# Row norms tile by tile: half-row squares, a shorter root, rows scaled and then turned

## What is computed

```python
def rms_norm(x, g):
    y = xf * lax.rsqrt(jnp.mean(xf * xf, axis=-1, keepdims=True) + NORM_EPS)
    return (y * g).astype(x.dtype)

for i in range(DEPTH):                         # first block
    h = rms_norm(x, ln_attn_g[i])              # a0, a1
    ...
    x = x + jnp.concatenate([y_diff, y_moba], axis=-1) @ w_out[i]
    x = x + conv_ffn(rms_norm(x, ln_ffn_g[i]), ...)      # f0, f1
for l in range(DEPTH):                         # second block
    h_l = _rmsnorm(x, g_pre[l]) * (1.0 + sc_l) + sh_l    # x0, x1
    h_c = _rmsnorm(xc, g_pre[l]) * (1.0 + sc_c) + sh_c   # c0, c1
    ...
    xc = xc + gt_c * _rmsnorm(out_c, g_post[l])          # layer 0 only
    x = x + gt_l * _rmsnorm(out_l, g_post[l])
```

## Time and profile before

| | us |
|---|---|
| median of 3 runs | 2309.98 |
| lowest, highest | 2309.71, 2314.76 |
| the profiled execution's own time | 2309.95 |
| its span in the trace | 2307.9 |
| PE busy | 2138.2 (93%) |
| DVE, ACT, POOL busy | 1321.8, 963.7, 555.7 |

### The profile page before, as it was taken

How to read it: one execution, slowest core, us unless ns; L and a number is a source line. 1 busy time by engine, 2 the same in 40 slices (tenths; PEclk the granted TensorE clock), 3 DMA queues, 4 the chain that set the end, 5 groups by cost and what they waited for, 6 DMA issues and landing times.

```text
span 2307.9 us, 31382 instructions
## 1 busy us (share of the span) xinstructions
PE 2138.2 (93%) x12074; PEld 1829.8 (79%) x12074; DVE 1321.8 (57%) x2200; ACT 963.7 (42%) x1602; POOL 555.7 (24%) x323
## 2 busy tenths in 40 slices
PE   7888998988999899999999999999989788989998
PEld 6668897766999688877887788888768688878997
DVE  5735666674777415638434456867361667565464
ACT  4434554443555424353323453232342553435443
POOL 1413333242333311011211002322231111320432
PEclk9979999988999999999999999999989899999999
DMA  9334665321455422212122115534323323341543
GB/s 250 126 136 167 232 217 201 128 91 65 160 180 190 133 92 73 82 46 73 65 95 87 47 37 175 182 102 138 120 78 126 101 83 110 110 147 46 174 146 129
DMA packets 79066, 285.00 MB, mean 123 GB/s; under 512 B 8822, under 2 KB 9730, under 8 KB 78920
## 3 DMA queue, kind: packets, MB, share of 16 engines
q1 hardware_dynamic: 70560, 256.15, 32.8%
q10 hardware_dynamic: 6072, 18.73, 2.3%
q0 software_dynamic: 2288, 8.13, 1.3%
HBM read 277.14 MB, written 5.83 MB: 123 GB/s over the span
## 4 chain that ended last, share of the span: by engine, by line
PE 40%; DVE 9%; ACT 4%; issue 2%; POOL 0%; POOLq 0%; DVEq 0%; ACTq 0%
PE pb L830 8%; PE pb L832 8%; PE pb L831 8%; PE pb L842 3%; PE pb L844 3%; PE pb L843 3%; PE pb L848 2%; PE pb L1156 2%; PE pb L1137 1%; ACT SPH L1277 1%; DVE GW L2105 1%; DVE SPL L1815 1%; PE pb L1053 1%; PE pb L1097 1%; DVE ATT L2133 1%
## 5 line engine op out<-in xcount | busy, mean ns | idle before, releaser
L1815 DVE TENSOR_TENSOR SPL<-RAW,SPH 128x1024 fp32r<-128x1024 f32 (+1 forms) x291 | 416.2, 1437 | 479.5 <-ACT SPH L1277 443.2
L2392 POOL TENSOR_TENSOR SPL<-RAW,SPH 128x1024 fp32r<-128x1024 f32 x171 | 418.6, 2450 | 1112.4 <-ACT SPH L1277 998.8
L830 PE MATMUL pb<-HTH,SPH 128*128 128x256 f32 (+1 forms) x1984 | 647.0, 326 | 8.1 <-DVE SPL L1815 3.9
L831 PE MATMUL pb<-HTL,SPH 128*128 128x256 f32 (+1 forms) x1984 | 636.9, 321 | 0.0
L832 PE MATMUL pb<-HTH,SPL 128*128 128x256 f32 (+1 forms) x1984 | 636.7, 321 | 0.0
L1277 ACT ACTIVATE SPH<-RAW 128x1024 fp32r<-128x1024 f32 x462 | 476.6, 1048 | 287.7 <-PE pb L844 130.2
L830 PEld LDWEIGHTS pb<-HTH,SPH 128*128 128x128 f32 x1984 | 381.7, 192 | 42.5 <-issue 14.1
L831 PEld LDWEIGHTS pb<-HTL,SPH 128*128 128x128 f32 x1984 | 382.1, 193 | 26.9
L832 PEld LDWEIGHTS pb<-HTH,SPL 128*128 128x128 f32 x1984 | 381.5, 192 | 27.1
L842 PE MATMUL pb<-SPH,HTH 128*128 128x512 f32 x544 | 222.0, 408 | 18.5 <-DVE SPL L1815 8.8
L844 PE MATMUL pb<-SPL,HTH 128*128 128x512 f32 x544 | 217.0, 399 | 0.0
(11 more groups left out here) (271 smaller groups left out, 2957.9 us busy)
## 6 DMA issues: line engine op xcount, KB each, us to landing
RAW<-in_w_up SPq DMA_DIRECT2D x88, 512.0 KB, 4.3
RAW<-in_wa SPq DMA_DIRECT2D x64, 512.0 KB, 3.2
RAW<-in_w_in SPq DMA_DIRECT2D x48, 512.0 KB, 5.3
RAW<-in_wmg SPq DMA_DIRECT2D x48, 512.0 KB, 3.2
RAW<-in_wbr SPq DMA_DIRECT2D x48, 512.0 KB, 3.2
RAW<-in_w_down SPq DMA_DIRECT2D x44, 512.0 KB, 3.5
RAW<-in_w_ada SPq DMA_DIRECT2D x24, 512.0 KB, 4.8
ARAW<-in_w_ada ACTq DMA_DIRECT2D x24, 512.0 KB, 4.0
```

Of the source, the lines that this page charges most:

```text
L830: T.matmul(o, wh[:, kt, :], xh[:, kt, n0:n1], start=kt == 0, stop=False)
L831: T.matmul(o, wh[:, kt, :], xl[:, kt, n0:n1], start=False, stop=False)
L1815: W.tensor_tensor(lo, raw, hi.bitcast(F32), SUB).then_inc(*dve.tick(s["lo_dve"], ("u", u)))
L2392: G.tensor_tensor(lo, raw, hi.bitcast(F32), SUB).then_inc(*pool.tick(s["lo_pool"], ("u", u)))
```

## The change

- **Squares.** Steps `sq`: a tile's sum of squares is taken in two halves of 512 columns, on ACT, as soon as each half is ready (for a0 and c0 the second half on DVE).
- **Root.** One root per tile on 128x1: an operation on the first half's sum, then eight in a chain once the second half's sum is there (before: eleven for two tiles). The same for `x_out`.
- **Scaling, then turning.** DVE scales columns 0 to 511 of a tile by its root, ACT the rest (for tile 0 of f0 and f1 ACT scales all), into XN. Steps `nt`: PE turns the 16 blocks of 128x128 by a transpose against the identity. Steps `nh`: HTH and HTL are written from PSUM. For x0, c0 and c1 ACT now writes HTH straight from PSUM, with DVE doing the scale and shift once more for the low part, and the low parts shared by DVE and POOL; x1 keeps its division of labour.
- **Last products tile by tile** (`group_by_tile`): the second output group of the attention, the last LAG = 3 down products, the first projection group of layer 1 (its tile 0 ahead of the turns of a1's tile 1) and the second w2 group, so that squares, roots and turns of one tile stand beside the products of another.
- **Second block, layer 0**: the group of context values gv comes first, context tiles ahead of x's tiles, with x0's turns between; the decay rank, gk and gq follow.
- Down products follow the up products by 3 tiles instead of 2, AH and AL have 4 buffers instead of 3. `ahead` puts splits on POOL. Loading TRI, the mask and the context moves from the start into the feed-forward network of layer 0. `x_half` multiplies by GB, `x_out` adds AFX to the first half in one operation with the scaling; XS goes out in four DMAs instead of two.

In all, PE has as many instructions as before, DVE 51 more, ACT 8 more; 9 weight splits go from DVE to POOL.

The core of the diff:

```diff
-PF = 2
+PF, LAG = 2, 3
...
+    def group_by_tile(self, key, name, g, tiles, src, both=0):
+        for i in range(both):
+            u = self.get_w(name, g * 4 + i)
+            self.add("gn", key, i, u, tiles, src, True)
+            self.put_w(u)
+            yield
+        us = [self.get_w(name, g * 4 + i) for i in range(both, 4)]
+        for t in tiles:
+            for i, u in enumerate(us):
+                self.add("gn", key, both + i, u, (t,), src, t == tiles[-1])
+                if t == tiles[-1]:
+                    self.put_w(u)
+                    self.ahead()
+                yield
+    def ahead(self):
+        was = list(self.split_on)
+        self.split_on[:] = (1,)
+        self.split_upto(self.gets - 1 + PF)
+        self.split_on[:] = was
+    def squares(self, tag, i):
+        for half in range(2):
+            self.add("sq", tag, i, half)
+    def root(self, tag, i):
+        self.add("root", tag, i, 0)
+        self.add("root", tag, i, 1)
+        self.add("xn", tag, i)
...
+    def qkv_first(self, ring):
+        for t in range(2):
+            self.take(ring, ("qkv", 1, 0, t))
+        for n, _ in enumerate(self.group_by_tile(("qkv", 1, 0), "w_in1", 0, (0, 1), ("a1",))):
+            if n == 3:
+                self.turns("a1", 1)
+                self.evict("a1", range(8), 1)
+            yield
...
+        tag = f"f{l}"
+        for t in range(2):
+            self.add("res1", l, 0, t)
+            self.give(("wo", l, 0, t))
+            self.add("sq", tag, t, 0)
+        for t in range(2):
+            self.take((2, 3), ("wo", l, 1, t))
+        for n, _ in enumerate(self.group_by_tile(("wo", l, 1), f"w_out{l}", 1, (0, 1), ("Y", l), 1)):
+            if n == 3:
+                self.add("res1", l, 1, 0)
+                self.give(("wo", l, 1, 0))
+                self.add("sq", tag, 0, 1)
+                self.add("root", tag, 0, 0)
+        self.add("res1", l, 1, 1)
+        self.give(("wo", l, 1, 1))
+        self.add("root", tag, 0, 1)
+        self.add("sq", tag, 1, 1)
+        self.add("xn", tag, 0)
+        self.root(tag, 1)
+        self.nt_take(tag, HI4)
+        for i in range(2):
+            self.turns(tag, i)
...
+    def down_end(self, l):
+        tag, first = "x0" if l else "a1", FF_TILES - LAG
+        us = [self.get_w(f"w_down{l}", first + i) for i in range(LAG)]
+        for i, t in ((0, 0), (1, 0), (0, 1), (2, 0), (1, 1), (2, 1)):
+            self.add("down", l, first + i, us[i], (t,))
+            if t:
+                self.put_w(us[i])
+                self.ahead()
+            if (i, t) == (2, 0):
+                for half in range(2):
+                    self.add("res2", l, 0, half)
+                    self.give(("dn", l, 0, half))
+                    self.add("sq", tag, 0, half)
+        self.root(tag, 0)
+        for half in range(2):
+            self.add("res2", l, 1, half)
+            self.give(("dn", l, 1, half))
+        if l:
+            self.squares(tag, 1)
+            self.root(tag, 1)
+            return
+        self.nt_take(tag, LO4, 0)
+        self.turns(tag, 0)
+        self.evict(tag, range(4), 0)
...
+            for t in (2, 3):
+                self.take(ALL8, ("gv", l, 0, t))
+            self.nt_take("x0", ALL8)
+            for t in (0, 1):
+                self.take(ALL8, ("gv", l, 0, t))
+            for n, _ in enumerate(self.group_by_tile(("gv", l, 0), f"wgv{l}", 0, (2, 3, 0, 1), H)):
+                if n == 3:
+                    for i in range(2):
+                        self.turns("x0", i)
+                    self.evict("x0", range(8))
+                    self.add("spill_x")
+                    self.add("wdec", l)
+            values(0)
...
+                t = tlist[n // 4]
+                self.add("x_out", l, t)
+                self.give(("w2", l, 1, t))
+                if not last and t < 2:
+                    self.squares("x1", t)
+                    self.root("x1", t)
+            elif not last and n == 13:
+                self.nt_take("x1", LO4)
+                for i in range(2):
+                    self.turns("x1", i)
+                self.evict("x1", range(4))
+                self.squares("c1", 0)
+                self.evict("x1", range(4, 6))
+        if last:
+            return
+        self.evict("x1", range(6, 8))
+        for n, _ in enumerate(self.gla_queries(1, ("x1",))):
+            if n == 0:
+                self.root("c1", 0)
+            elif n == 1:
+                self.squares("c1", 1)
+                self.root("c1", 1)
+        self.nt_take("c1", ALL8)
+        for i in range(2):
+            self.turns("c1", i)
+        self.evict("c1", range(8))
...
+    def sq(tag, i, half):
+        if half and tag in SQUARED_BY_DVE:
+            return
+        t, c = NORMS[tag][i], slice(half * 512, half * 512 + 512)
+        k.rows_ready(act, tag, t, half)
+        xn_free(act, k, tag, i)
+        A.activation(xn_tile(sb, tag, i)[:, c], sb["XS"][:, t, c], ACT.Square, scale=1.0,
+                     accum_out=sb["SS"][:, 2 * t + half:2 * t + half + 1]).then_inc(
+            *act.tick(s["norm_act"], ("sq", tag, i, half)))
+    def xn(tag, i):
+        t, c = NORMS[tag][i], slice(0 if (tag, i) in SCALED_BY_ACT else 512, 1024)
+        act.wait_ge(s["norm_dve"], ("rs", tag, i))
+        A.activation(xn_tile(sb, tag, i)[:, c], sb["XS"][:, t, c], ACT.Copy, scale=sb["NW"][:, i, 8:9]).then_inc(
+            *act.tick(s["norm_act"], ("xn", tag, i)))
...
+    def nt(tag, b, i):
+        P, x = bank(nt_bank(tag, b, i)), xn_tile(sb, tag, i)
+        for kt in (b, b + 4):
+            if kt < 4 and (tag, i) not in SCALED_BY_ACT:
+                pe.wait_ge(s["norm_dve"], ("xn", tag, i))
+            else:
+                pe.wait_ge(s["norm_act"], ("xn", tag, i))
+            at = nt_block(tag, kt, i)[0].start + (0 if tag in BY_TILE else i * 128)
+            m = turn(P[:, at:at + 128], x[:, kt * 128:(kt + 1) * 128])
+        m.then_inc(*pe.tick(mm, ("nt", tag, b, i)))
...
+    def root_step(signal, w, n, out, *names):
+        dve.wait_ge(*dve.last)
+        W.scalar_tensor_tensor(out=w[:, 7:8], in0=w[:, 6:7], scalar=w[:, n:n + 1], in1=w[:, 6:7], op0=MUL,
+                               op1=MUL).then_inc(*dve.tick(signal))
+        dve.wait_ge(*dve.last)
+        W.scalar_tensor_tensor(out=out, in0=w[:, 7:8], scalar=3.0 if n == 2 else -3.0, in1=w[:, 6:7], op0=ADD,
+                               op1=MUL).then_inc(*dve.tick(signal, *names))
...
+    def root(tag, i, part):
+        n, t, w = s["norm_dve"], NORMS[tag][i], sb["NW"][:, i, :]
+        if part == 0:
+            dve.wait_ge(s["norm_act"], ("sq", tag, i, 0))
+            root_open(n, w, sb["SS"][:, 2 * t:2 * t + 1])
+            dve.wait_ge(s["norm_dve" if tag in SQUARED_BY_DVE else "norm_act"], ("sq", tag, i, 1))
+            root_guess(n, w, sb["SS"][:, 2 * t + 1:2 * t + 2])
+            root_step(n, w, 0, w[:, 6:7], ("rp", tag, i))
+            return
+        dve.wait_ge(n, ("rp", tag, i))
+        root_step(n, w, 1, w[:, 6:7])
+        root_step(n, w, 2, w[:, 8:9], ("rs", tag, i))
...
         dve.wait_ge(*dve.last)
-        rsqrt(o, ("xr", l, t), SSO[:, 1, t:t + 1], SSO[:, 0, t:t + 1], 1.0 / 1024, 1)
-        dve.wait_ge(o, ("xr", l, t))
         dve.wait_ge(*k.read(("w2", l, 0, t)))
-        for hf in range(2):
-            dve.wait_ge(*k.read(("gr", l, t // 2, hf)))
-        W.scalar_tensor_tensor(out=x[:, 512:1024], in0=k.P(name)[:, :], scalar=SSO[:, 1, t:t + 1],
-                               in1=GB[:, t // 2, 512:1024], op0=MUL, op1=MUL).then_inc(*dve.free(*k.read(name)))
-        W.scalar_tensor_tensor(out=x[:, 0:512], in0=x[:, 0:512], scalar=SSO[:, 1, t:t + 1],
-                               in1=GB[:, t // 2, 0:512], op0=MUL, op1=MUL).then_inc(*dve.tick(o))
+        dve.wait_ge(s["x_back"], 16 * (l + 1))
+        W.scalar_tensor_tensor(out=x[:, 0:512], in0=x[:, 0:512], scalar=r, in1=sb["AFX"][:, t, 0:512], op0=MUL,
+                               op1=ADD).then_inc(*dve.tick(o, ("x", l, t, 0)))
+        dve.wait_ge(*k.read(("gr", l, t // 2, 1)))
+        W.scalar_tensor_tensor(out=x[:, 512:1024], in0=k.P(name)[:, :], scalar=r, in1=sb["GB"][:, t // 2, 512:1024],
+                               op0=MUL, op1=MUL).then_inc(*dve.free(*k.read(name)))
         dve.wait_ge(*dve.last)
-        dve.wait_ge(*k.read(name))
-        dve.wait_ge(s["x_back"], 16 * (l + 1))
-        W.tensor_tensor(x, x, sb["AFX"][:, t, :], ADD).then_inc(*dve.tick(o, ("x", l, t)))
+        W.tensor_tensor(x[:, 512:1024], x[:, 512:1024], sb["AFX"][:, t, 512:1024], ADD).then_inc(
+            *dve.tick(o, ("x", l, t, 1), ("x", l, t)))
```

563 lines of the change are left out of this document (285 added, 278 removed).

## The result

The changed kernel takes 2318.23 us (median of 10 runs, 2317.11 to 2320.08), the kernel before, run beside it, 2311.81 (10 runs, 2309.71 to 2314.76). The ratio is 1.0029, interval 1.0019 to 1.0039: slower by 0.29%. The forecast was 2287, its range 2274 to 2302. It was wrong in size and in direction.

The account below looks back on a forecast made before the run. PE's matmuls (busy 2138.2 of 2307.9 us) bound the kernel, so only idle and half clock could be won. 4.0 + 0.8 + 5.7 + 11.5 + 1.6 + 0.3 - 1.0 = 22.9; 2309.95 - 22.9 = 2287, range 2274 to 2302.

Parts of the forecast that it names:

- a1: Norm ahead of layer 1's projections: gain 0.8 us, bounds -2 and +8, with splits late behind the second tile's scaled rows.
- x0: Norm ahead of the second block: less PE idle and no wait for AL, gain 5.7 us, bounds 3 and 8.
- the end: After the last square: fewer root steps, a half-width addition and a smaller last DMA, gain 1.6 us.
- f0 and f1: Norms ahead of both layers' up products: shorter root path, 2.0 us each, 4.0 together, bounds 1 and 9.
- the start: Start with a0's norm: one transfer gone, POOL splits before building bias rows, gain 0.3 us, bounds -1 and +1.6.
- the network of layer 0: Feed-forward loops: LAG and the fourth AH/AL buffer change nothing, as long as PE stays at its 128x512 pitch.
- c0: Context norm, placed in layer 1's attention: extra DVE and ACT work, loss of 1.0 us, bounds -3 and +1.
- x1 with c1: Norms at the end of the first block 2 layer: query groups start earlier, gain 11.5 us, bounds 6 and 14.
- rival B: At a1, x0, f0, f1 and x1: splits come in time, clock holds, gains 36.9 us, 2273; chance 0.14.
- C: Rival: half clock behind the turns at f0, f1, a1, x0 and c1 loses 8 us, 2295; chance 0.18.
- E: Rival: slower, POOL's added splits hold DVE 21 us in dense stages, c0 adds 4.4, 2313; chance 0.05.
- same: Whole kernel: a time not distinguishable from no change, within about 0.3% (6.9 us); chance 0.07.

Follow-up runs that it names:

- e10: e5 with the TRI, mask and context loads back at the start and the mask's cast ahead of the attention: 2294.99 us.
- e1: Changed kernel with low parts after the first four weight splits on DVE until layer 0's attention, not every third on POOL: 2308.04 us.
- e2: Changed kernel with the doubled modulation steps of layer 0's feed-forward network at tiles 7 and 8 instead of 8 and 9: 2310.06 us.
- e3: Changed kernel with two more weight splits ahead of tile 1's squares and root at a1 and x0: 2305.98 us.
- e5: Changed kernel with the edits of e1, e2 and e3 together: 2286.56 us, ratio 0.9888 to the kernel before.
- e9: e5 with all of c0's norm moved from layer 1's projections and attention into its feed-forward network: 2276.74 us.
- e7: e5 with c0's column blocks written out one per step of the attention instead of two: 2286.12 us.
- e8: e5 with the two splits taken during the last w2 tile on DVE instead of POOL: 2284.74 us.
- e4: Changed kernel with plain products against the identity in place of the transposes: 2327.87 us.
- after: The changed kernel itself, without any follow-up edit: 2318.23 us, ratio 1.0029 to the kernel before.
- e6: e5 with one more split ahead of c0's squares and roots in layer 1's projections: 2287.10 us.

## Why the prediction was wrong, step by step

- **What bounds.** Held: with as many turns as products only idle and half clock could be won, and the DG waits went away in full. The prediction looked for gains in the holes that exist, and for losses mostly in the same places. It did not walk through the stages in which PE had no hole. Of the sum's terms a1, x0 and the end came out right, f0 and f1 under-sized; the start, the network of layer 0, c0, and x1 with c1 failed, and they are 7.4, 13.5, 6.9 and 7.1 us of error.
- **Start, 0.3, measured a loss of 7.1. The failed step** is "POOL splits before it builds the bias rows: 0.3". Two splits do stand ahead of the bias rows (10.51 and 22.79), but the costly two stand behind their round trip through DRAM (9.36 us). The trip was to be read in the trace of before (8.11 us of idle), and that splits now follow it from the new kernel's order. And the moved load, which the prediction took for one of several small things, is worth 9.6 (e10). Two terms of about ten, a cost (12.6, e1) and a gain, both put at next to nothing.
- **Feed-forward, "nothing, as long as PE stays at its 128x512 pitch", measured a loss of 13.5 in layer 0. The failed step, and the largest.** The condition was stated and not examined. The doubling at tiles 8 and 9 made PE wait 6.00 us for AROW; e2 took 8.2 us of it back by moving the doubling one tile. Another 4.2 are the loads and the mask's cast, moved here from the start (e10). Nothing in PE's pitch before could show it; the order of ACT and PE around tiles 8 and 9 would have.
- **f0 and f1, 4.0, measured 4.1 and 4.5, 8.6 together.** Mechanism right; under-sized by half. The first turn came at T + 3.2 and the first up product at T + 6.8 instead of 8.5 (T here the last output product). The mis-sized term is the evictions: the sum let them run to T + 8.5 ahead of the up products; they ran under them. And the transposes take 3.57 us, against 5.12 for the products, which the sum left out.
- **a1, 0.8, measured a loss of 0.2; x0, 5.7, measured 5.6.** Right place, right mechanism (splits behind the scaled rows on ACT), shown by e3: 5.7 and 4.9 us. For a1 the sum had T + 23.3 against 24.1; it came to 24.24 against 24.04. With the splits in time (e5) it is 5.5 and 12.0, rival B's direction.
- **c0, a loss of 1.0 with bounds -3 and +1, measured 7.9. Mis-sized term.** I added up c0's work (4.4 us on DVE and ACT), took a part of it, and placed it all in the attention, though its squares and roots stand in the projections (2.1 of the loss). There the chain of two roots and scalings occupies DVE from 445.37 to 451.66 and ACT waits with the next split; in the attention the turns wait another 6.24 for HVC. The work was not the price; the position in the order was. e9 gives back 9.8 by moving it. What inside the attention holds HVC stays open, since e7 did not settle it.
- **x1 and c1, 11.5, measured 4.4. Mis-sized term.** Tile 3 with the turns in it ended as forecast to 0.5 us (1689.4 against 1689.9). The last query copy is at 1730.41 - 14.6 = 1715.8, forecast 1707.5, a gain of 3.9 instead of 12.2; PE's own query products end 6.9 earlier, 5.3 less than forecast. Late low parts (POOL's splits are 2.5, e8), ACT's evictions and the clock at 0.50 until 1719.5 are what the traces show there; all were in the prediction's warnings, not in its sum. The step "c1's turns and evictions follow as before" failed too: the faster turns ran into a new wait of 4.02 us for c1's low parts, a net 2.7.
- **End, 1.6, measured 1.5.** Right.
- **The rivals.** C is refuted where it was looked at (e4, the windows of f0 and f1). E named a mechanism that exists (DVE held for 2.3 us beside a POOL split, and after's 1702.11) and an outcome on the right side; but e1 to e3 win back more than the whole loss elsewhere, without its 21 us of held DVE in the dense stages. e8 puts the one place where it was tried at 2.5 us. (By E's own figures eight held splits beside c0's 4.4 us are enough to reach no change, not ten, and the parts named for "same" add up to 0.085, not 0.07.) No rival held the two mechanisms that decided: a queue behind a round trip, and a producer and its consumer moved into one step.

Without the two faults of order (e1 and e2, 18.4 us measured singly) after would be at about 2300, inside the range; e5 has them out together with e3.

## What to carry to other kernels

- Of an engine that takes over work, read what stands ahead of the new work in its in-order list, waits included. A wait that cost nobody anything becomes everybody's when something needed is queued behind it.
- When a step is doubled or merged, look whether a producer on one engine and its consumer on another now fall into the same step; one step between them was worth 8 us here.
- A stage's price is not the added work but the delay of the next thing in the list that PE needs. Work that two other orders did not hide in a dense stage (e6, e7) could be put whole into a stage where PE is the bound (e9). Before stages of two kernels are compared between two products, the same work must lie ahead of both: here twelve products did not, which makes a1 look 2 us worse in the table and x0 1 us. A total that comes out right (e5, 2286.56 against 2287) proves no term of the sum.

## What the runs showed of the hardware

- A 128x128 float32 transpose is one record and a product of the same size two, at the same pitch: from the first of 16 to the next stage 3.57 us against 6.38 in e4 (5.12 in the kernel before).
- The clock came back behind turns alone: 0.50 at 190.90, 1.00 from 194.40.
- Of two holes of 2.67 and 2.68 us at the same place of the program one was followed by a clock of 1.00 and one by 0.58 for 7 us, 3.1 us of difference. Shifts of that size between two kernels need a look at PEclk before they are put down to an edit.
- Root steps of 0.16 and 0.22 us on DVE took 2.31 and 2.26 beside POOL's two splits (4.69 us). That agrees with the Trainium skill's GPSIMD Engine Reference (Specifications), by which the SBUF interfaces are shared with VectorE.
- POOL's issue of a DMA that needs an earlier one landed blocked its list for 9.36 us (8.11 in the kernel before).
- A load of over 1 MB at the start (TRI, mask, context) let a weight chunk be split only at 46.31 instead of 39.25 us (e10, e5).
